# Condition and bias vectors loaded as rows in three modulation stages, and a recurrence-output stage whose per-unit chain is ordered within the unit

## The reference, cut to what matters

```python
mod  = (silu(c)     @ w_ada + b_ada).reshape(B, 1, 6, 1024)      # w_ada: 1024 x 6144
modc = (silu(c_ctx) @ w_ada + b_ada).reshape(6, 1024)
h    = rmsnorm(x) * g * (1 + scale) + shift
```

## Time and profile before

| | us |
|---|---|
| median of 3 runs | 5544.89 (5543.59 to 5551.47) |
| the profiled execution, its own time | 5546.77 |
| its span, first to last instruction | 5545.0 |
| `first_norm`, from 5.9 | to 96.5 |
| `recurrence_outputs`, from 1592.4 | to 1765.3 |
| `choose_tokens` with a modulation, from 3684.0 | to 3788.2 |

### The profile page before, as it was taken

How to read it: one execution, slowest core, us unless ns; L and a number is a source line. 1 busy time by engine, 2 the same in 40 slices (tenths; PEclk the granted TensorE clock), 3 DMA queues, 4 the chain that set the end, 5 groups by cost and what they waited for, 6 DMA issues and landing times. The chain is left out here.

```text
span 5545.0 us, 90112 instructions
## 1 busy us (share of the span) xinstructions
PE 4746.2 (86%) x39216; PEld 3716.7 (67%) x39216; DVE 1649.8 (30%) x2466; ACT 960.2 (17%) x1600; POOL 1018.9 (18%) x801
## 2 busy tenths in 40 slices
PE   6989887788875869999969899867999799995997
PEld 3868777788853457787745577745786366773776
DVE  1037344444422223322330234350000212434001
ACT  2115012222211020000020223120000211322111
POOL 2210214433411112232200000111111001010111
PEclk9989988899986989999979799978999898997999
DMA  7210200000034311111100100148775110002996
GB/s 252 87 36 1 57 29 5 3 4 4 4 121 162 100 31 42 49 45 45 45 19 27 38 1 1 31 152 317 253 246 169 61 35 18 1 27 86 346 314 227
DMA packets 320251, 483.97 MB, mean 87 GB/s; under 512 B 42025, under 2 KB 197547, under 8 KB 310739
## 3 DMA queue, kind: packets, MB, share of 16 engines
q1 hardware_dynamic: 299954, 403.78, 21.3%
q0 software_dynamic: 17696, 67.29, 4.5%
q10 hardware_dynamic: 2304, 8.39, 0.4%
HBM read 422.80 MB, written 56.62 MB: 86 GB/s over the span
## 5 line engine op out<-in xcount | busy, mean ns | idle before, releaser
L2244 PE MATMUL l_in_ps<-l_mixT,l_in_w 128*128 128x512 f32 (+1 forms) x672 | 258.8, 548 | 38.6 <-DMA l_in_w<-in_w_in_dram 38.6
L3390 PEld LDWEIGHTS l_experts_pG<-l_experts_xT,l_experts_wg 128*128 128x128 f32 x2048 | 261.8, 194 | 15.5 <-issue 13.3
L3390 PE MATMUL l_experts_pG<-l_experts_xT,l_experts_wg 128*128 128x160 f32 (+1 forms) x2048 | 266.0, 292 | 1.6 <-ACT l_experts_xT L3442 1.6
L3390 PE MATMUL l_experts_pU<-l_experts_xT,l_experts_wu 128*128 128x160 f32 (+1 forms) x2048 | 258.7, 287 | 0.0
L3390 PEld LDWEIGHTS l_experts_pU<-l_experts_xT,l_experts_wu 128*128 128x128 f32 x2048 | 255.6, 191 | 0.0
L3412 PE MATMUL l_experts_pY<-l_experts_wd,l_experts_hid 128*128 128x512 f32 x512 | 230.6, 598 | 21.6 <-DVE l_experts_hid L3454 20.5
L2244 PEld LDWEIGHTS l_in_ps<-l_mixT,l_in_w 128*128 128x128 f32 x672 | 129.1, 192 | 167.9 <-issue 124.9
L131 PE MATMUL mlp_ps<-h_hi,mlp_w_hi 128*128 128x512 f32 x512 | 200.4, 391 | 32.2 <-POOL mlp_w_lo L119 32.2
L131 PE MATMUL mlp_ps<-mlp_hid_hi,mlp_w_hi 128*128 128x512 f32 x512 | 203.8, 398 | 25.4 <-DVE mlp_hid_lo L2183 25.4
L131 PE MATMUL mlp_ps<-mlp_hid_lo,mlp_w_hi 128*128 128x512 f32 x512 | 202.9, 396 | 0.0
L131 PE MATMUL mlp_ps<-mlp_hid_hi,mlp_w_lo 128*128 128x512 f32 x512 | 202.3, 395 | 0.0
(11 more groups left out here) (608 smaller groups left out, 9911.0 us busy)
## 6 DMA issues: line engine op xcount, KB each, us to landing
l_experts_wg<-in_w_gate_dram SPq DMA_DIRECT2D x32, 2048.0 KB
l_experts_wu<-in_w_up_dram SPq DMA_DIRECT2D x32, 2048.0 KB, 14.5
l_experts_wd<-in_w_down_dram SPq DMA_DIRECT2D x32, 2048.0 KB, 13.5
rec_out_w_ada<-in_w_ada_dram SPq DMA_DIRECT2D x24, 1024.0 KB, 7.9
l_choose_w_ada<-in_w_ada_dram POOLq DMA_DIRECT2D x24, 1024.0 KB, 16.1
mlp_w<-in_w_mlp_up_dram SPq DMA_DIRECT2D x32, 512.0 KB, 3.9
mlp_w<-in_w_mlp_down_dram SPq DMA_DIRECT2D x32, 512.0 KB, 3.4
s_acc<-l_choose_zero SPq DMA_DIRECT2D x18, 512.0 KB, 5.1
```

The source lines that it names most:

```text
L2244: mm = nc.tensor.matmul(ps[:, m % 2, c, 0:n], w[:, m % 2, k], hT[:, k, t0:t0 + n], start=(k == 0), stop=(k == KT - 1))
L3390: mm = nc.tensor.matmul(ps[:, f // 2, f % 2 * S:f % 2 * S + S], w[:, b, k, f * P:(f + 1) * P], xT[:, b, k], start=(k == 0), stop=(k == KT ...
```

## The change

1. `Modulation`. Each condition is loaded as 8 rows of 128 elements and transposed by PE (`turn_conds`); `silu` reads PSUM and waits for the conditions alone. The bias goes, as 8 loads of 3 x 512 elements, straight into the rows of `rows` where the products will stand (the other rows are set to zero on DVE first, and the loads wait for that). `read_out` moves from ACT to DVE and adds the bias; behind the transposes `put_out` only copies.
2. `first_norm`: g is loaded by SP, ahead of the row tiles, as 8 rows, and transposed by PE.
3. `recurrence_outputs`: its four small vectors are loaded as rows too. ACT's affine step and DVE's weighing now belong to unit q itself, `bonus_of(q-1)` goes ahead of them; PE's lists keep their order, with `turn` of a finished block put in one unit later. The second pass has four banks, four buffers of `yr` and four of g; the first four loads of g stand behind all `w_ada` loads in SP's queue.
4. `choose_tokens`: PE turns back the lists before the modulation's rows, and DVE's three `read_out` stand behind its work on the lists.

```diff
     def load_small(self, eng):
-        with self.nc.allow_non_contiguous_dma("vectors into columns"):
-            for j, v in enumerate(self.conds):
-                eng.dma_start(self.cond_sb[:, :, j], v.rearrange("(k p) -> p k", p=P)).then_inc(self.small_loaded, 16)
+        for j, v in enumerate(self.conds):
+            eng.dma_start(self.cond_rows[j * KT:(j + 1) * KT], v.rearrange("(k p) -> k p", p=P)
+                          ).then_inc(self.cond_loaded, 16)
+        eng.wait_ge(self.padded, 2)
+        for q in range(4):
             for j in range(2):
-                eng.dma_start(self.bias[:, :, j], self.b_ada.rearrange("(k p) -> p k", p=P)
-                              ).then_inc(self.small_loaded, 16)
+                eng.dma_start(self.rows[32 * q + j:32 * q + j + 1],
+                              self.b_ada.rearrange("(b q c) -> q b c", q=4, c=self.W)[q:q + 1]
+                              ).then_inc(self.bias_loaded, 16)
...
+        self.nc.vector.memset(self.rows[:], 0.0).then_inc(self.padded, 1)
...
-        act.wait_ge(self.small_loaded, 64)
+        act.wait_ge(self.cond_turned, 1)
...
-    def read_out(self, act, b):
+    def read_out(self, dve, b):
         e = b * KT + KT - 1
-        act.wait_ge(self.w_used[e % self.ring], e // self.ring + 1)
-        self.nc.scalar.activation(self.rows[:, b], self.banks[b], ACT.Copy).then_inc(self.read, 1)
+        dve.wait_ge(self.bias_loaded, 128)
+        dve.wait_ge(self.w_used[e % self.ring], e // self.ring + 1)
+        self.nc.vector.tensor_tensor(self.rows[:, b], self.banks[b], self.rows[:, b], ALU.add).then_inc(self.read, 1)
...
                 for b in range(1, m.BLOCKS):
-                    m.add_bias(dve, b)
+                    m.read_out(dve, b)
+                    m.put_out(dve, b)
...
-                for q in range(2):
-                    sp.dma_start(g[:, q], part(g_dram, q)).then_inc(g_loaded[q], 16)
                 side.load(sp)
+                for q in range(4):
+                    sp.dma_start(g[:, q], part(g_dram, q)).then_inc(g_loaded[q], 16)
...
                     if q:
-                        weigh(q - 1)
-                    if q >= 2:
-                        bonus_of(q - 2)
-                weigh(NU - 1)
-                bonus_of(NU - 2)
+                        bonus_of(q - 1)
+                        for b in side_blocks(q - 1):
+                            side.read_out(dve, b)
+                    dve.wait_ge(affine, q + 1)
+                    chain(nc.vector.tensor_tensor(bon[:, q % 2], a[:, q % 2], rkv[:, 4 + m, t], ALU.mult))
...
-                if side is not None:
-                    for b in range(side.BLOCKS):
-                        side.turn(pe, b)
                 pe.wait_ge(chosen, 1)
...
                     for b in range(side.BLOCKS):
-                        side.add_bias(dve, b)
+                        side.read_out(dve, b)
+                    for b in range(side.BLOCKS):
+                        side.put_out(dve, b)
```

More of the change, by code:

```diff
@@ L264, in _ @@
                 m.load_small(pool)
-                with nc.allow_non_contiguous_dma("a vector into columns"):
-                    pool.dma_start(g[:], g_vec.rearrange("(k p) -> p k", p=P)).then_inc(g_loaded, 16)
                 for u in own[1]:
@@ L283, in _ @@
                     nc.scalar.activation(h[0][:, k, t0:t0 + n], whole[:, u % 4, 0:n], ACT.Copy).then_inc(hi_done, 1)
-                for b in range(1, m.BLOCKS):
-                    m.read_out(act, b)
             @block.tensor
@@ L324, in _ @@
                 last.then_inc(diag_done, 1)
[L325 to L326 removed]
+                m.read_out(dve, 0)
+                m.put_out(dve, 0).then_inc(biased, 1)
+                dve.wait_ge(g_read, 1)
                 dve.wait_ge(biased, 1)
@@ L1850, in sums @@
                 def sums(q):
+                    pe.wait_ge(bon_done, q + 1)
+                    if q:
+                        pe.wait_ge(bonus, q)
+                    nc.tensor.matmul(pb[:], ones64[:], bon[:, q % 2], start=True, stop=True).then_inc(bon_sum, 1)
                     pe.wait_ge(squared, q + 1)
@@ L1893, in _ @@
                     mm.then_inc(spread, 1)
-                for b in range(side.BLOCKS):
-                    side.turn(pe, b)
             @block.scalar
             def _(act):
-                act.wait_ge(loaded, 144)
                 side.silu(act)
                 act.wait_ge(vec_done, 2)
-                def rest(q):
-                    m, c = units[q]
-                    for b in side_blocks(q):
-                        side.read_out(act, b)
-                    act.wait_ge(added, q + 1)
-                    nc.scalar.activation(a[:, q % 2], a[:, q % 2], ACT.Identity, scale=vec[:, 4, m:m + 1],
-                                         bias=vec[:, 5, m:m + 1]).then_inc(affine, 1)
                 for q, (m, c) in enumerate(units):
```

132 lines of the change are left out of this document (69 added, 63 removed).

## The result

The changed kernel takes 5457.06 us (median of 4 runs, 5451.50 to 5458.48) where the kernel before took 5544.31 beside it (4 runs, 5543.59 to 5551.47). The ratio is 0.9838, 95% interval 0.9821 to 0.9855: 87.3 us faster, where 5453 us and 92.4 were predicted. The profiled execution took 5458.48 us with a span of 5456.5.

What follows compares the result with a forecast made beforehand. TensorE is busy 86% of the span, so gains come only where it waits. `first_norm` -7.3, `recurrence_outputs` -79.6 and `choose_tokens` -5.5 sum to -92.4 from 5544.9, giving 5453 us, range 5436 to 5482.

Steps and rivals of the forecast that it cites:

- `first_norm`, -7.3: Stage `first_norm`: bytes arriving earlier, less small costs of issue, read-out and a reordered end, make it 7.3 us shorter.
- the lost bytes, 8.95 us: `first_norm`, 10 to 25 us: single-element loads cost 3.75 MB of transfer; without them all work moves forward 8.95 us.
- The +1.0 for the order of the end: End of `first_norm`: the second block's copy no longer lies under the first transposes, costing 1.0 us.
- Units, -68: `recurrence_outputs`: earlier start and units without waits bring the last product's end from 1729.1 to 1661, 68 us earlier.
- The wait is paid twice: `recurrence_outputs` units: TensorE's 4.54 us wait for DVE costs itself and also a halved clock in what follows.
- Rival (a): `recurrence_outputs` units: TensorE's clock stays low, total 5502 us, or 5477 if low half the time; chance 0.12.
- End and second pass, -11.6: `recurrence_outputs` after the last product: 24.6 us instead of 36.2, from earlier scaling and shorter steps.
- The 1.9 us a step: Second pass of `recurrence_outputs`: POOL's steps 1.9 us apart with four banks and buffers, against 2.8 on average before.
- `choose_tokens`, -5.5: Stage `choose_tokens`: 6.4 us gained from lost bytes, 0.9 us given back at the end, 5.5 us shorter.
- The rule on transfers confined to few engines: Bias row loads: each on at most 3 DMA engines, eight in a row an estimated 16 us; expected to change little.
- Rival (d): Bias rows land so late that read-outs on DVE hold up sums and means; 5545 us and above, chance 0.01.

Runs made afterwards that it cites:

- the second profile: The changed kernel run and profiled once more with no edit, 5454.6 us (5 runs).
- the filled gap: Changed kernel with affine step and weighing back in their old late place, plus 17 useless TensorE products ahead of each bonus sum; 5500.3 us.

## Why the prediction was right

- *`first_norm`, -7.3*: measured -7.0. The step "the lost bytes, 8.95 us" was right in kind (9.3 ns of an engine for each element); the first product moved by 7.6 and the last by 8.1. The +1.0 for the order of the end measured 1.1, at the low clock that the kernel before had there too (0.52); in the second profile, with the clock up, it is 0.15.
- *Units, -68*: from the stage's start to the last product's end it is now 67.0 us (1584.98 to 1651.98), before 136.6 (1592.51 to 1729.1): -69.6. "The wait is paid twice" is shown by the filled gap. A unit is 7.5 us on the mean, as forecast; the loads bind by a little, with 9.7 us of short waits of weight loads in all, 1.5 of TensorE's products. Rival (a) would have had the clock fall in them; from 1599 on it stayed at 1.00. The Trainium skill's second failure mode (TensorE: Matmul & The Clock Gate), a swing of the clock through brief idling between groups, did not appear in these units.
- *End and second pass, -11.6*: measured 25.8 us instead of 36.2, -10.4. The term mis-sized is the first: VectorE starts scaling 6.1 us after the last product's end (1658.06), not 5.0, since the last bonus sum waits (0.4 us) and the spreading takes 1.98 us, not 1.2, at a granted clock of 0.50. In the second profile the clock is 1.00 there, the spreading takes 1.09, VectorE starts after 5.2, and the end and second pass take 24.8 us, -11.3. The 1.9 us a step was the right number, but the reason that I gave (the pace where nothing else holds GpSimd) was not: it is the exclusion of the two engines, and with the operand in PSUM a step is 1.45 to 1.55.
- *`choose_tokens`, -5.5*: measured -6.4; the last product came 7.5 us nearer instead of 6.4, and the end cost 1.1 (0.9 forecast).
- *The rule on transfers confined to few engines* (the Trainium skill, DMA: Bandwidth & Descriptors, Rules for kernel authors) gave an estimate of 16 us for the eight bias rows in a row. That they would run one behind the other was the prediction's own step, not the page's. In `recurrence_outputs` they were issued within 3.6 us (0.52 us each) and landed 5.3 us later on the median, 6.5 at most: all were there 10.1 us after the first issue at the latest. They overlap, and the first read-out, at 1619.3, came 22 us after that. On how many engines each ran, no view shows. Rival (d) had no ground.
- *What the sum left out*: -3.1 and +8.0 us in unchanged stretches, half of the latter shown to be the granted clock. It is the whole miss of 5 us between -93.4 and -88.5. In the second profile the stages give -93.9 and the other stretches -6.0 and +7.5; its span is 5452.6, 92.4 us below that of before. That this is the forecast to the tenth is luck, since the sum held nothing for these stretches.

## What to carry to other kernels

Load vectors as rows and turn them on TensorE: a full share of DMA engines with low GB/s is the sign that something without bytes is being moved. Before counting the gain of a removed wait, read the granted clock of what follows it; a chain moved one unit earlier here gave 31 to 34 us of waiting and 24 to 27 of clock. Where VectorE and GpSimd share a step, look for a VectorE operation that ends just after GpSimd's, and keep one of its inputs in PSUM.

## What was not expected of the hardware

- An operation of VectorE with two inputs in SBUF takes 1.20 us beside GpSimd and 0.75 alone; with one of them in PSUM 0.75 beside GpSimd too.
- Eight loads of single elements behind each other stop GpSimd twice at their issue, for 7.1 to 14.8 us in the three stages (11.1 and 13.6 in `recurrence_outputs`); four did not.
- The same stretch of unchanged instructions (last layer, heads to projection) takes 346.1 to 357.3 us in thirteen kernels' traces, and the same within 0.2 us in two executions of one kernel. A longer stretch (`gates` to `recurrence_outputs`) moved by 3.6 us between the same two executions.
